# A three-layer transformer on one core: difference attention with its score products issued further ahead, and short score tiles that share a bank

## The reference, cut to what matters

```
def diff_attention(q1, q2, k1, k2, v, lam):
    ...
        a1 = masked_softmax(jnp.einsum('bqhd,bkhd->bhqk', qb1, k1).astype(jnp.float32) * scale, mask)
        a2 = masked_softmax(jnp.einsum('bqhd,bkhd->bhqk', qb2, k2).astype(jnp.float32) * scale, mask)
        p = a1 - lam * a2
        return jnp.einsum('bhqk,bkhd->bqhd', p.astype(v.dtype), v)
```

## Time and profile before

| | |
|---|---|
| median of 3 runs | 2665.61 us (2664.06 to 2671.1) |
| the profiled execution's own time | 2668.06 us |
| its span, first to last instruction | 2666.3 us |
| mean granted TensorE clock | 0.921 of full |
| difference attention, first scores to first matmul of the projection | 1988.82 to 2116.25 us |
| the other causal attentions (latent; sparse; forgetting; branches) | 275 to 324; 344 to 385; 1036 to 1079; 1146 to 1262 us |

### The profile page before, as it was taken

One profiled execution on the slowest core, in us unless ns is written; L12 is line 12 of the kernel. 1 busy time (PEld: TensorE's weight loads), 2 busy tenths in 40 slices (PEclk: granted clock), 3 DMA queues, 4 the chain that ended last, 5 costly groups with the idle time before them and its releaser, 6 DMA issues.

```text
span 2666.3 us, 31087 instructions
## 1 busy us (share of the span) xinstructions
PE 2362.9 (89%) x11372; PEld 1863.9 (70%) x11372; DVE 1290.3 (48%) x2286; ACT 1070.6 (40%) x1888; POOL 683.4 (26%) x419
## 2 busy tenths in 40 slices
PE   5788889998899979989968999998986678999997
PEld 4551568886688767766757888886764566788886
DVE  3667553445699834345544433323336554434233
ACT  3222563435588825235334332222125533333221
POOL 2225122230000022410323332323620141333232
PEclk9799999988799989998978999998997788899998
DMA  4100002312699931120211222221210011222221
GB/s 179 48 24 16 32 26 98 111 64 95 248 397 385 362 107 56 63 83 6 72 48 48 92 98 95 95 103 48 86 64 1 32 64 48 68 99 93 97 95 56
DMA packets 71942, 260.11 MB, mean 98 GB/s; under 512 B 7984, under 2 KB 8112, under 8 KB 71408
## 3 DMA queue, kind: packets, MB, share of 16 engines
q1 hardware_dynamic: 66960, 239.41, 25.5%
q0 software_dynamic: 2672, 11.30, 1.1%
q10 hardware_dynamic: 2160, 7.42, 0.7%
HBM read 246.54 MB, written 11.56 MB: 97 GB/s over the span
## 4 chain that ended last, share of the span: by engine, by line
PE 72%; DVE 9%; issue 8%; ACT 6%; POOL 3%; DMA 2%; SPq 0%; POOLq 0%; DVEq 0%; ACTq 0%
PE ps L490 14%; PE ps L492 14%; PE ps L491 14%; PE ps L1010 2%; PE ps L544 2%; PE ps L2378 2%; PE ps L2379 2%; PE ps L2380 2%; PE ps L525 2%; PE ps L526 2%; PE ps L527 2%; PE ps L1029 2%; PE ps L993 1%; PE ps L689 1%; ACT Sb L1097 1%
## 5 line engine op out<-in xcount | busy, mean ns | idle before, releaser
L437 POOL TENSOR_TENSOR wl<-raw,wh 128x1024 fp32r<-128x1024 f32 x133 | 321.3, 2416 | 1080.0 <-ACT wh L432 806.8
L432 ACT ACTIVATE wh<-raw 128x1024 fp32r<-128x1024 f32 x316 | 331.1, 1056 | 618.2 <-PE ps L492 581.4
L490 PE MATMUL ps<-hh,wh 128*128 128x512 f32 (+1 forms) x1192 | 479.0, 402 | 5.0 <-DVE wl L437 3.5
L492 PE MATMUL ps<-hh,wl 128*128 128x512 f32 (+1 forms) x1192 | 466.9, 392 | 0.0
L491 PE MATMUL ps<-hl,wh 128*128 128x512 f32 (+1 forms) x1192 | 466.7, 392 | 0.0
L437 DVE TENSOR_TENSOR wl<-raw,wh 128x1024 fp32r<-128x1024 f32 x183 | 246.0, 1350 | 423.0 <-ACT wh L432 416.0
L490 PE MATMUL ps<-act,wh 128*128 128x512 f32 (+1 forms) x752 | 293.2, 390 | 27.1 <-POOL wl L437 15.5
L491 PE MATMUL ps<-act,wh 128*128 128x512 f32 (+1 forms) x752 | 290.4, 386 | 0.0
L492 PE MATMUL ps<-act,wl 128*128 128x512 f32 (+1 forms) x752 | 289.8, 385 | 0.0
L490 PEld LDWEIGHTS ps<-hh,wh 128*128 128x128 f32 (+1 forms) x1192 | 225.5, 189 | 61.0 <-issue 11.6
L491 PEld LDWEIGHTS ps<-hl,wh 128*128 128x128 f32 (+1 forms) x1192 | 225.4, 189 | 51.7 <-issue 5.7
(11 more groups left out here) (417 smaller groups left out, 4027.5 us busy)
## 6 DMA issues: line engine op xcount, KB each, us to landing
raw<-d_w SPq DMA_DIRECT2D x278, 512.0 KB, 3.5
raw_x<-d_moe SPq DMA_DIRECT2D x84, 512.0 KB, 6.5
raw<-d_moe SPq DMA_DIRECT2D x84, 512.0 KB, 6.6
d_xs<-Sb POOLq DMA_DIRECT2D x7, 514.0 KB, 6.3
Xb<-d_xs ACTq DMA_DIRECT2D x7, 514.0 KB, 5.1
d_ys<-rows ACTq DMA_DIRECT2D x7, 512.0 KB, 6.6
area<-d_mem POOLq DMA_DIRECT2D x3, 1024.0 KB, 5.1
xT<-d_x SPq DMA_DIRECT2D x8, 256.0 KB, 4.9
```

What stands on the lines that cost most here:

```text
L432: me.e.activation(hi, raw, ACT.Copy).then_inc(*me.done("wh", m))
L437: me.e.tensor_tensor(lo, raw, hi.bitcast(F32), ALU.subtract).then_inc(*me.done("wl", m))
L490: me.e.matmul(bank[0:m, 0:n], wh[:, c], hi, start=k == 0, stop=False)
L492: mm = me.e.matmul(bank[0:m, 0:n], wl[:, c], hi, start=False, stop=last)
```

## The change

1. `score_at` now depends on h. In a causal pair, block 1 of h = 0 and block 1 of h = 1 (256 columns each) share one bank, so a pair needs five banks. `score_banks` takes all of them before the first product, and `score_banks_back` gives them back. The order of products is `score_order`: (0,0), (0,1), (2,0), (2,1), (1,0), (3,1), (3,0), (1,1) as (block, h). The last product waits for the fifth, which writes the same bank, and readers of either block 1 wait for the last. Where a tile has two products (the forgetting attention), both of one tile now stand one behind the other; before, they alternated with the other head's. The cross attentions keep four banks, but take them at once too.
2. The second map of the difference attention gets two buffers (`K.other`; the second lies in `K.S_h`, the memory of the normed input, so that memory counts as free only after the stage).
3. PE makes the scores of head n+1 in step n, ahead of the turns of head n-1; two banks are set apart (`turns`) for turned packs and turned-back results; value products go to `K.ACC`, each head's behind `scaled` of the head before.
4. DVE's order in step n is: maxima of n, norm squares of n-2, combination of n-1, gain of n-3, scaling of n-2, copy for n-1. ACT's is: squares of n-2, exponentials of n, copies for n-1, rounding of n-3.
5. ACT's root and DVE's reciprocal are replaced by two POOL instructions on 128x4 (multiply and add, then power -0.5).

```diff
         self.pools[pool].append((self.plan.slot[key], after))
+
+    def set_apart(self, pool, other, n):
+        self.pools[other] = deque(self.pools[pool].popleft() for _ in range(n))
+
+    def put_back(self, pool, other):
+        self.pools[pool].extend(self.pools.pop(other))
 
...
 
 
-def score_at(it, i):
+def score_at(it, i, h):
+
     for g, group in enumerate(groups(it)):
-        at = 0
+        at = 256 * h if it["causal"] and g == 1 else 0
         for n in group:
             if n == i:
                 return g, slice(at, at + it["width"](i))
             at += it["width"](n)
+
+
+def score_order(it):
+
+    if it["causal"]:
+        return [(0, 0), (0, 1), (2, 0), (2, 1), (1, 0), (3, 1), (3, 0), (1, 1)]
+    return [(i, h) for i in range(NQ) for h in range(2)]
+
+
+def score_banks(K, me, it, key):
+    for g in range(len(groups(it))):
+        for h in range(2):
+            if it["causal"] and g == 1 and h:
+                K.plan.slot[("S", *key, 1, 1)] = K.plan.slot[("S", *key, 0, 1)]
+            else:
+                me.take("ps", "S", *key, h, g)
+
+
+def score_ready(it, h, g):
+    return (1, 1) if it["causal"] and g == 1 else (h, g)
+
+
+def score_banks_back(me, it, key, read):
+    for g, group in enumerate(groups(it)):
+        for h in range(2):
+            if it["causal"] and g == 1:
+                if h:
+                    me.give("ps", ("S", *key, 1, 1), (read, *key, 0, 1), (read, *key, 1, 1))
+            else:
+                me.give("ps", ("S", *key, h, g), (read, *key, h, group[-1]))
 
 
...
 def products_pe(K, me, a, p, pair):
     it = pair[0]
-    for g, group in enumerate(groups(it)):
-        banks = [K.banks[me.take("ps", "S", a, p, h, g)] for h in range(2)]
-        for h in range(2):
-            for k in pair[h]["tok"]:
-                me.wait_ge(*k)
-        for i in group:
-            c = score_at(it, i)[1]
-            mats = [pair[h]["mats"](i) for h in range(2)]
-            for m in range(len(mats[0])):
-                for h in range(2):
-                    mm = me.e.matmul(banks[h][:, c], *mats[h][m], start=m == 0, stop=m == len(mats[0]) - 1)
-                    if i == group[-1] and m == len(mats[0]) - 1:
-                        mm.then_inc(*me.done("S", a, p, h, g))
-        for h in range(2):
-            me.give("ps", ("S", a, p, h, g), ("max" if it["mask"] else "exp", a, p, h, group[-1]))
+    score_banks(K, me, it, (a, p))
+    for h in range(2):
+        for k in pair[h]["tok"]:
+            me.wait_ge(*k)
+    for i, h in score_order(it):
+        g, c = score_at(it, i, h)
+        mats = pair[h]["mats"](i)
+        if it["causal"] and (i, h) == (1, 1):
+            me.wait_ge("S", a, p, 0, 1)
+        for m, (l, r) in enumerate(mats):
+            mm = me.e.matmul(K.bank("S", a, p, h, g)[:, c], l, r, start=m == 0, stop=m == len(mats) - 1)
+        if i == groups(it)[g][-1]:
+            mm.then_inc(*me.done("S", a, p, h, g))
+    score_banks_back(me, it, (a, p), "max" if it["mask"] else "exp")
 
 
...
     K.lam, K.gs = K.mis[:, 2:3], K.mis[:, 3:4]
 
 
 def diff_products_pe(K, me, n, it):
-    for g, group in enumerate(groups(it)):
-        banks = [K.banks[me.take("ps", "S", "diff", n, part, g)] for part in range(2)]
-        for k in it["tok"]:
-            me.wait_ge(*k)
-        for i in group:
-            c = score_at(it, i)[1]
-            for part in range(2):
-                (l, r), = it["mats"][part](i)
-                mm = me.e.matmul(banks[part][:, c], l, r, start=True, stop=True)
-                if i == group[-1]:
-                    mm.then_inc(*me.done("S", "diff", n, part, g))
-        for part in range(2):
-            me.give("ps", ("S", "diff", n, part, g), ("max", "diff", n, part, group[-1]))
+    score_banks(K, me, it, ("diff", n))
+    for k in it["tok"]:
+        me.wait_ge(*k)
+    for i, part in score_order(it):
+        g, c = score_at(it, i, part)
+        (l, r), = it["mats"][part](i)
+        if (i, part) == (1, 1):
+            me.wait_ge("S", "diff", n, 0, 1)
+        mm = me.e.matmul(K.bank("S", "diff", n, part, g)[:, c], l, r, start=True, stop=True)
+        if i == groups(it)[g][-1]:
+            mm.then_inc(*me.done("S", "diff", n, part, g))
+    score_banks_back(me, it, ("diff", n), "max")
 
 
...
-        bank = K.banks[me.take("ps", "T", "diff", n, pk)]
+        bank = K.banks[me.take("turns", "T", "diff", n, pk)]
         me.wait_ge(*normed)
         for j, i0, c0 in pack:
             for i in range(i0, NQ):
                 c = c0 + 128 * (i - i0)
                 tp = me.e.transpose(bank[:, c:c + 128], S[:, i, 128 * j:128 * j + 128], K.ident)
         tp.then_inc(*me.done("T", "diff", n, pk))
-        me.give("ps", ("T", "diff", n, pk), ("PT", "diff", n, pk))
+        me.give("turns", ("T", "diff", n, pk), ("PT", "diff", n, pk))
     me.alias("turned", "diff", n)
 
 
...
 
 
 def second_free(n):
-    return [("comb2", n - 1)] if n else [("end", "pe", (("ffn", 0), 2))]
+    return [("comb2", n - 2)] if n >= 2 else [("end", "pe", (("ffn", 0), 2))]
+
+
...
+def diff_values_pe(K, me, m):
+    it = K.i_diff[m]
+    if m:
+        me.wait_ge("scaled", m - 1)
+    me.wait_ge("val", "vd", m)
+    for i in range(NQ):
+        for j in range(i + 1):
+            c = place(it, j, i)
+            me.wait_ge("PT", "diff", m, pack_of(it, j)[0])
+            mm = me.e.matmul(K.ACC[:, 128 * i:128 * i + 128], K.PTf[:, c:c + 128], it["v"](j), start=j == 0, stop=j == i)
+    mm.then_inc(*me.done("pv", "diff", m))
+
+
+def diff_features_pe(K, me, m):
+    bank = K.banks[me.take("turns", "feat", m)]
+    me.wait_ge("scaled", m)
+    for i in range(NQ):
+        tp = me.e.transpose(bank[:, 128 * i:128 * i + 128], K.tan("diffn", "dsq", m)[:, 128 * i:128 * i + 128], K.ident)
+    tp.then_inc(*me.done("feat", m))
+    me.give("turns", ("feat", m), ("gained", m))
 
 
 def diff_pe(K, me):
     h = K.h("n6")
     heads_pe(K, me, "dqk", "od_w_in_2", h, K.i_dqk, "n6", 3)
     values_pe(K, me, "vd", K.i_vd)
+    me.set_apart("ps", "turns", 2)
+    for n in range(2):
+        diff_products_pe(K, me, n, K.i_diff[n])
+    for n in range(1, 10):
+        if n + 1 < 8:
+            diff_products_pe(K, me, n + 1, K.i_diff[n + 1])
+        if n < 9:
+            diff_turn_pe(K, me, n - 1, K.i_diff[n - 1], K.first[(n - 1) % 2], ("comb2", n - 1))
+            diff_values_pe(K, me, n - 1)
+        if n >= 2:
+            diff_features_pe(K, me, n - 2)
+    me.put_back("ps", "turns")
     me.alias("hfree", "n7")
-    for n in range(10):
-        if n < 8:
-            diff_products_pe(K, me, n, K.i_diff[n])
-        if 1 <= n < 9:
-            diff_turn_pe(K, me, n - 1, K.i_diff[n - 1], K.first[(n - 1) % 2], ("comb2", n - 1))
-        if n >= 2:
-            bank = K.banks[me.take("ps", "feat", n - 2)]
-            me.wait_ge("scaled", n - 2)
-            for i in range(NQ):
-                tp = me.e.transpose(bank[:, 128 * i:128 * i + 128], K.tan("diffn", "dsq", n - 2)[:, 128 * i:128 * i + 128], K.ident)
-            tp.then_inc(*me.done("feat", n - 2))
-            me.give("ps", ("feat", n - 2), ("gained", n - 2))
-        if 1 <= n < 9:
-            it, m = K.i_diff[n - 1], n - 1
-            bank = K.banks[me.take("ps", "att", m)]
-            me.wait_ge("val", "vd", m)
-            for i in range(NQ):
-                for j in range(i + 1):
-                    c = place(it, j, i)
-                    me.wait_ge("PT", "diff", m, pack_of(it, j)[0])
-                    mm = me.e.matmul(bank[:, 128 * i:128 * i + 128], K.PTf[:, c:c + 128], it["v"](j), start=j == 0,
-                                     stop=j == i)
-            mm.then_inc(*me.done("pv", "diff", m))
-            me.give("ps", ("att", m), ("scaled", m))
     me.alias("end", "pe", "diff")
     sandwich_pe(K, me, "x7", "od_w_out_2", 0, K.parts(0, 8, 8, "dt"), "mem2")
+
+
...
+def diff_squares_act(K, me, m):
+    i = me.take("ta", "diffn", "dsq", m)
+    ss = K.st_d("sd", "diff", m)[:, 16:20]
+    me.wait_ge("pv", "diff", m)
+    for q in range(NQ):
+        c = slice(128 * q, 128 * q + 128)
+        me.e.activation(K.ta[:, i, c], K.ACC[:, c], ACT.Square, accum_out=ss[:, q:q + 1]).then_inc(
+            *me.done("diffn", "dsq", m) if q == NQ - 1 else me.done())
+    me.give("ta", ("diffn", "dsq", m), ("feat", m))
 
 
...
+    for n in range(11):
+        if 2 <= n < 10:
+            diff_squares_act(K, me, n - 2)
+        if n < 8:
+            diff_exp_act(K, me, n, K.i_diff[n], K.first[n % 2], first_free(n), 0)
+            diff_exp_act(K, me, n, K.i_diff[n], K.other[n % 2], second_free(n), 1)
         if 1 <= n < 9:
             diff_turned_copy(K, me, n - 1, K.i_diff[n - 1], pt_free("diff", n - 1, first_free(0)))
-        if n < 8:
-            diff_exp_act(K, me, n, K.i_diff[n], K.first[n % 2], first_free(n), 0)
-            diff_exp_act(K, me, n, K.i_diff[n], K.S[:, 1, :, :], second_free(n), 1)
-        if n >= 2:
-            m = n - 2
...
```

(70 more changed lines are left out.)

108 lines of the change are left out of this document (48 added, 60 removed).

## The result

The changed kernel takes 2648.05 us (median of 5 runs, 2642.97 to 2653.96), the kernel before 2666.47 us beside it (5 runs, 2664.06 to 2671.1). The ratio is 0.9925, 95% interval 0.9907 to 0.9943: 20 us faster (15 to 25). I had said 2645.0, between 2633 and 2659. Direction and size came out, but the terms did not: the stage gave more than I said, the shared helpers took more, and the two misses nearly cancel. So the closeness of the total is in part luck.

A forecast was written before the change was run, and what follows sets the result against it. PE time bounds the whole program, but a loop through all engines bounds the difference attention. Terms -28.7 (difference), +4.8 (latent), +3.8 (forgetting), -0.5 (rest) sum to -20.6 us, giving 2645.0 us, range 2633 to 2659.

The forecast's parts named there:

- The bound: Difference attention: no engine is full in one head's 15.80 us; a loop through all engines binds.
- The period, 10.1 us: Difference attention, steady time per head: DVE's 9.35 us plus 0.75 for waits and stalls, ends 9.6 and 11.75.
- the loop is the largest of two things: Difference attention: the period is set by DVE's own work, 9.35 us, or the chain between combinations, 9.0 us.
- the norm's chain: Difference attention, combination to combination through turns, copies, values, squares and norm: 9.0 us at full clock, 11.75 at half.
- Start and end: Difference attention: second combination ends at 2018.5, five periods of 10.1, a last of 9.4, then the tail; gain 28.7 us.
- the tail: Difference attention, last turns to the projection: 9.2 us, where the old kernel took 9.43.
- The root on POOL: Difference attention: POOL's two root instructions take 0.7 us with hand-overs, bounds 0.2 and 2.5, hidden in the periods.
- The rival that it holds DVE: Difference attention: POOL's root stops DVE's combination, period about 9.8 + r, total about 2684 us at r = 6; chance 0.06.
- Half clock: Rival, difference attention: PE stays at the lower clock through turns and values, period 11.75, total 2657.7 us; chance 0.16.
- Latent attention, +4.8 us: DVE's second batch waits for all products, about 1.1 us in each of 4 pairs; three scores start 0.2 later; bounds 2 and 7.
- Forgetting attention, +3.8 us: Same-half products cost 0.65 us a pair, the second pair's scores wait 1.5 us for block 1; bounds 1.5 and 5.
- The rest, -0.5 us: Sparse attention unharmed, branches gain a spare bank for turned packs: -0.5 us for all, bounds -3 and +1.

The follow-up runs named there:

- not_ahead: Changed kernel with PE's score products of head n+1 issued behind the turns and value products of head n-1, not ahead; ratio 1.0049, 2682.02 us.
- root_on_act: stage_only with the root back on ACT and the reciprocal back on DVE in place of POOL's two instructions; ratio 0.9978 to the kernel before, 2661.07 us.
- third_buffer: stage_only with a third buffer for the first map of the difference attention; ratio 0.9878 to the kernel before, 2636.45 us.
- root_padded: Changed kernel with four more unused 128x4 powers on POOL behind each head's root; ratio 0.9929 to the kernel before, 2651.12 us.
- third_buffer_copy: third_buffer with the second turned pack copied by ACT too; ratio 0.9879 to the kernel before, 2638.53 us.
- banks_when_needed: Changed kernel with a causal pair's banks in the shared attentions taken at first use, not all five up front; ratio 0.9884 to the kernel before, 2638.30 us.
- helpers_only: Changed kernel's shared attentions (five banks a pair) with the difference attention as before; ratio 1.0023 to the kernel before, 2676.11 us.
- short_earlier: Changed kernel with its last two causal score products swapped; ratio 0.9916 to the kernel before, 2646.57 us.
- stage_only: Changed kernel's difference attention with the shared attentions as before (six banks a pair); ratio 0.9886 to the kernel before, 2638.25 us.

## Why the prediction was right, and where not

**The bound.** Right: a loop through all engines, broken by giving each head's parts different steps. not_ahead and root_on_act show that both the order of PE and the root's place are needed; without the first the whole gain goes, without the second three quarters of the stage's.

**The period, 10.1 us.** Measured 9.47. The step that failed is "the loop is the largest of two things". DVE's own work was 8.96 by its rows, of which 0.3 is a hold, against my 9.35; the norm's chain is 8.88 against 9.0. Neither binds: the third, through POOL's rounding rest, does. I had put 0.75 us on top for such holds without following them round a loop. The result lies below my lower end of 9.6, and near it only because the third loop happens to be 0.1 us longer than my 9.35.

**Start and end.** From the first scores to the second head's turns I had 28.65 us (1989.85 to 2018.5); it took 26.34. The five periods behind them took 47.0 us in place of 50.5. The last period took 11.27 us for 9.4 and the tail 10.48 for 9.2: with no scores left to issue, PE idles 4.90 and 4.25 us and turns and multiplies for the most part at the lower level (0.65 and 0.76 over the two stretches). I had taken the pace of the earlier trace rows, where 20 value products took 2.76 us after an idle of 5.72; now they took 4.08 and 3.60. This term is a matter of chance: third_buffer has the same idles there, 4.90 and 4.25, and its value products took 2.76 and 2.94. Sum of the four: 2.3 + 3.5 - 1.9 - 1.3 = 2.6 us shorter than my 97.75. The scores begin 1.4 us later behind the last turns before them (I had 1.0). That makes the stage's 30.9 us against my 28.7.

**The root on POOL.** The two instructions took 1.29 us from start to end, inside the bounds of 0.2 and 2.5; I had 0.7. It is covered in the period. The rival that it holds DVE took the 1.26 us of L3335 in the earlier trace rows, held by POOL's L680, as a sign that the root would do the same. It doesn't: in both kernels the holder is the 128x512 rounding rest, never the root.

The Trainium skill ("SBUF — State Buffer", section "SBUF: two separate sides") says that GpSimd and a DVE operation in a 2-port mode or with two SBUF inputs share a port pair, and that whichever starts first holds it for its whole instruction. The 28 holds by L686 agree with it, and so do the powers of 1.55 us in root_padded. What doesn't agree: the third addition there started in the middle of a power and kept its 0.61 us, and all four kept 1.94. Here the measurement decides.

**Half clock.** This rival did not come: the granted clock is 1.00 in the steady period. third_buffer_copy and root_on_act show it one edit away.

**Latent attention, +4.8 us.** (My own terms, 4 x 1.1 + 3 x 0.2, give 5.0.) Measured +6.0 between the two profiles. Over the others the stage is 69.7 to 70.3 us in six kernels that have it as before and 74.4 to 75.5 in three that have it as changed, so single profiles can't tell 4.8 from 6.0. Of each pair's 1.5 us, 1.03 is scores to turns (I had 1.1) and about 0.5 the later start of scores (I had 0.2): banks_when_needed takes that half away. The idle of 2 us that I expected before each turn is split: 0.81 us before the sums are spread, 0.72 before the turns.

**Forgetting attention, +3.8 us.** Measured +2.0: first pair's scores to the third's 14.84 to 16.59 us, third to fourth 10.12 to 10.23, and 0.2 in the last pair. TensorE's rows in the changed kernel, against the earlier trace rows:
```profile
1044.52 4.66 PE L1030 MATMUL ps<-area 64*128 64x128 f32 x32
1050.91 4.66 PE L1030 MATMUL ps<-area 64*128 64x128 f32 x32 [1.72 <-POOL area L3137]
```
The later start is 1.72 us (I had 1.5). The row names POOL's L3137, but in the program that instruction makes the factor of the third pair; the second pair's was ready before the stage. What it waits for is the bank of the short tiles: in helpers_only the same wait, 1.68 us, is put to DVE's maxima (L1117), as I had reckoned. The 0.65 us a pair for products on the same half was mis-sized: 0.1 to 0.2 here. short_earlier shows when it does cost, 1 us, with two tiles of one half in a row.

**The rest, -0.5 us.** Wrong, and outside its bounds: the branches lost 3.7 us between the two profiles (not shown to be more than scatter, see banks_when_needed) and two cross attentions 0.95 each from first scores to turns (7.66 to 8.61, 7.74 to 8.69); the sparse attention gained 1.0. I had only counted the spare bank at the turns and not what it costs to take all banks before the first product. Sum of the terms as measured: -30.9 + 6.0 + 2.0 - 1.0 + 3.7 + 1.9 = -18.3 us, beside -18.9 between the two profiles and -20 (-15 to -25) by the runs. Between the same two profiles, stretches that no edit touches differ by up to 4.5 us (the one ahead of the latent attention), some up and some down, so the agreement is closer than the terms are.

**Open.** helpers_only lost 6.2 us (2.7 to 9.3) where the difference of the changed kernel and stage_only is 10.4; the two intervals overlap and more can't be told. The second map's second buffer and the two banks set apart were never taken out by themselves, so what they give of the stage's gain is not shown. The loop through L686 rests on rows of eight kernels; no run moved L686 by itself. The best ratio, third_buffer's 0.9878, is not separable from stage_only's 0.9886 by time. Its stage is 2.6 us shorter, but 2.1 of that lies in the last two stretches, where the idles are the same and the clock was granted otherwise; the third buffer itself shows for 0.5 us.

## What to carry to other kernels

When an engine seems full, take work from it: if the period doesn't move, the bound is elsewhere, and a short instruction that is longer than its twin is the place to look, together with what another engine ends at that moment. Take buffers in the order and at the time of their use; a pool emptied up front ties the first product to the last reader. A change to a shared helper is costed at each of its callers, and if only one stage needs it, only that stage should get it: here that is worth about 10 us of 30 (the changed kernel beside stage_only).

## What the runs showed of the hardware

A DVE instruction of 128x4 inside SBUF stood still for up to 0.7 us until POOL's 128x512 subtraction ended, while maxima that read PSUM ran beside it at their usual 0.69 us. A POOL power of 128x4 takes 1.01 us, not much less than a 128x512 subtraction (1.27), and held no DVE instruction. With idles of 0.83 and 1.64 us in a period of 9.47 PE kept the upper level (2.4 GHz); with one of 1.88 and one of 0.22 us in a period of 10.4 it was granted the lower one (1.2 GHz) for part of each. In the same kernel two such idles, 1.89 and 0.22 us, had stood in a period of 8.9 at the upper level, so the idles alone don't tell.
